# Issuing the next pair's probabilities and scores ahead of the turned outputs of pairs 0 and 1, and layer 1's gate rows behind two head units

## The reference, cut to what matters

```
mod = cond @ w_mod[l] + b_mod[l]                  # six vectors of 1024
h = rms_norm(x, norm_mix[l]) * (1 + sc_a) + sh_a
mq, mk, mv, dq, dk, dv = split(h @ w_in[l])       # 12 units of 256 columns
q, k = partial_rope(rms_norm(q)), partial_rope(rms_norm(k))
o_m = rms_norm(softmax(mq mk^T, causal) @ mv)     # 8 heads of 64
o_d = rms_norm((softmax_1 - lam * softmax_2) @ dv) # 4 double heads, values 128 wide
x = x + g_a * (concat(o_m, o_d) @ w_out[l])
h = rms_norm(x, norm_ffn[l]) * (1 + sc_f) + sh_f
x = x + g_f * ((silu(h @ w_gate[l]) * (h @ w_up[l])) @ w_down[l])
```

## Time and profile before

| what | value |
|---|---|
| median of 3 runs | 2172.64 us (2172.41 to 2173.16) |
| the profiled execution's own time | 2173.13 us |
| its span, first to last instruction | 2171.4 us |
| tensor engine (PE) busy | 2092.4 us, 96% |
| VectorE (DVE) busy | 875.6 us, 40% |
| ScalarE (ACT) busy | 374.7 us, 17% |
| mean granted clock of the tensor engine | 0.984 of full speed |
| layer 0's attention stage of the second block | about 1410 to 1557 us of the span |
| layer 1's attention stage of the second block | about 1790 to 1945 us of the span |

### The profile page before, as it was taken

The page is one execution under the profiler, slowest core; times in us unless marked ns, Lnnn a source line. Parts: engine busy times, 40 slices in busy tenths (PEclk is TensorE's granted clock), DMA queues, the critical chain, the costliest instruction groups (busy, mean ns, idle before and its releaser), DMA issues.

```text
span 2171.4 us, 37454 instructions
## 1 busy us (share of the span) xinstructions
PE 2092.4 (96%) x16270; PEld 1553.5 (72%) x16270; DVE 875.6 (40%) x1693; ACT 374.7 (17%) x899; POOL 74.5 (3%) x180
## 2 busy tenths in 40 slices
PE   8998999999999989999999999999999999999998
PEld 8786786887788867866653554388687768868786
DVE  1414525677734154242010000135566754454443
ACT  1312240000013122401010000133300012431000
POOL 3000000010000000020000000000000010000000
PEclk9999899999999998998999999999999999999999
DMA  9334234598563342327999999962568754333452
GB/s 261 97 98 153 90 126 151 182 322 277 194 197 98 97 160 78 126 79 235 348 312 377 345 347 326 315 212 97 176 238 291 265 182 151 98 117 120 154 174 97
DMA packets 333831, 421.44 MB, mean 194 GB/s; under 512 B 27222, under 2 KB 282148, under 8 KB 333668
## 3 DMA queue, kind: packets, MB, share of 16 engines
q1 hardware_dynamic: 312464, 352.96, 50.3%
q0 software_dynamic: 13408, 50.66, 6.6%
q10 hardware_dynamic: 7796, 15.43, 2.0%
HBM read 417.90 MB, written 1.05 MB: 193 GB/s over the span
## 4 chain that ended last, share of the span: by engine, by line
PE 84%; DMA 6%; DVE 4%; ACT 3%; ACTq 1%; issue 1%; SPq 0%; DVEq 0%
PE psum L1295 15%; PE psum L1327 13%; PE psum L1434 11%; PE psum L1302 9%; PE psum L1312 9%; PE psum L1494 5%; DMA ring<-in_w_up 4%; PE psum L1958 3%; PE psum L1565 3%; PE psum L1740 2%; PE psum L1339 2%; DMA ring<-in_ffn_w 2%; ACTq L653 1%; PE psum L1423 1%; PE psum L1507 1%
## 5 line engine op out<-in xcount | busy, mean ns | idle before, releaser
L1295 PE MATMUL psum<-xT,ring 128*128 128x256 f32 x1600 | 373.7, 394 | 6.8 <-ACT small L779 4.1
L1295 PEld LDWEIGHTS psum<-xT,ring 128*128 128x128 f32 x1600 | 312.1, 197 | 63.1 <-issue 7.0
L1312 PE MATMUL psum<-ring,arena 128*128 128x512 f32 x528 | 232.1, 593 | 0.0
L1302 PE MATMUL psum<-ring,xT 128*128 128x256 f32 (+2 forms) x960 | 201.1, 367 | 2.8 <-DVE arena L2466 2.1
L1302 PEld LDWEIGHTS psum<-ring,xT 128*128 128x128 f32 x960 | 170.6, 190 | 29.4 <-DVE arena L2466 2.7
L1312 PEld LDWEIGHTS psum<-ring,arena 128*128 128x128 f32 x528 | 97.9, 190 | 111.8 <-issue 111.6
L2145 DVE SCALAR_TENSOR_TENSOR arena<-arena,cond 128x512 f32<-128x512 f32 x168 | 126.2, 751 | 5.5
L1327 PEld LDWEIGHTS psum<-xT,ring 128*128 128x128 f32 x960 | 112.8, 194 | 20.7 <-issue 20.7
L1434 PE MATMUL psum<-ring,arena 128*32 128x256 f32 x2304 | 126.8, 379 | 0.7 <-DVE arena L2299 0.7
L1327 PE MATMUL psum<-oT,arena 128*128 128x128 f32 x960 | 117.4, 275 | 5.9 <-DVE arena L2160 5.8
L1327 PE MATMUL psum<-xT,ring 128*128 128x128 f32 x960 | 114.1, 278 | 6.0 <-DMA ring<-in_w_up 3.5
(11 more groups left out here) (414 smaller groups left out, 2518.4 us busy)
## 6 DMA issues: line engine op xcount, KB each, us to landing
ring<-in_w_in SPq DMA_DIRECT2D x80, 1024.0 KB, 5.5
ring<-in_exp_w SPq DMA_DIRECT2D x312, 256.0 KB, 6.2
arena<-in_w_mod POOLq DMA_DIRECT2D x48, 1024.0 KB, 9.2
ring<-in_ffn_w SPq DMA_DIRECT2D x33, 1024.0 KB, 7.3
arena<-in_exp_w SPq DMA_DIRECT2D x120, 256.0 KB, 7.1
ring<-in_w_gate SPq DMA_DIRECT2D x22, 1024.0 KB, 7.6
ring<-in_w_up SPq DMA_DIRECT2D x22, 1024.0 KB, 10.1
ring<-in_w_down SPq DMA_DIRECT2D x22, 1024.0 KB, 5.0
```

The lines of the kernel that those rows point to most:

```text
L1295: ins = pe.matmul(dst, w[:, k * 256 + c0:k * 256 + c0 + m], act_t[:, k, :], start=(k == 0), stop=(k == KT - 1))
L1302: ins = pe.matmul(dst, xT[:, k, t * P:t * P + P], w[:, k * 256 + c0:k * 256 + c0 + n], start=(k == 0), stop=(k == KT - 1))
L1312: ins = pe.matmul(psum[:, 4 + 2 * t + h, :], gT[:, s % 2, f * 256 + t * P:f * 256 + t * P + P], w2[:, f * D + h * 512:f * D + h * 512 + 51 ...
```

## The change

On the tensor engine, in both layers: `turn_probs2(l, 2)` and `scores2(l, 3)` go ahead of `turn_outs(l, 0)` and `weigh2(l, 1)`; `turn_probs2(l, 3)` goes ahead of `turn_outs(l, 1)` and `weigh2(l, 2)`. ScalarE's list follows: `keep_probs(l, 2)` ahead of `keep_outs(l, 0)`, `keep_probs(l, 3)` ahead of `keep_outs(l, 1)`. In layer 1 alone: `spread(1)` goes behind `project(1, 2)`, `keep_clock` stands ahead of that projection and has 6 products in place of 14, and ScalarE's `keep_rows(1)` goes behind the roots of the first two head units. VectorE, GpSimd and SP issue the same instructions in the same order. Line numbers from L1092 on are higher by 1 to 4 in the changed file.

```diff
                 act.preload_act_table_set("natural_log_exp_and_others")
-                keep_rows(l)
+                if l == 0:
+                    keep_rows(l)
...
                 square_heads(l, 1)
                 head_roots(l, 1)
+                if l == 1:
+                    keep_rows(l)
                 keep_heads(l, 0)
...
                 keep_heads(l, 6)
+                keep_probs(l, 2)
                 keep_outs(l, 0)
                 square_outs(l, 1)
-                keep_probs(l, 2)
                 out_roots(l, 1)
                 exp2(l, 3)
                 keep_values(l, 8)
                 keep_heads(l, 7)
+                keep_probs(l, 3)
                 keep_outs(l, 1)
                 square_outs(l, 2)
-                keep_probs(l, 3)
                 out_roots(l, 2)
...
+                del turned_last[:]
+                if l == 1:
+                    keep_clock(3, 6)
+                project(l, 2)
                 if l == 1:
                     spread(1)
-                    keep_clock(3, 14)
-                del turned_last[:]
-                project(l, 2)
                 turn_heads(l, 0)
...
                 turn_heads(l, 6)
+                turn_probs2(l, 2)
+                scores2(l, 3)
                 turn_outs(l, 0)
                 weigh2(l, 1)
-                turn_probs2(l, 2)
-                scores2(l, 3)
                 project(l, 8)
                 turn_heads(l, 7)
+                turn_probs2(l, 3)
                 turn_outs(l, 1)
                 weigh2(l, 2)
-                turn_probs2(l, 3)
                 project(l, 9)
```

## The result

The changed kernel took 2158.87 us (median of 5 runs, 2158.04 to 2160.52), the kernel before 2172.41 in the same series (5 runs, 2167.36 to 2173.16): ratio 0.9949, 95% interval 0.9936 to 0.9961. That is 11 us or 0.5% less at the ratio, and more than forecast; the time lies 2.5 us under the low end of the range. The two runs of the kernel before that joined the first three were 2167.36 and 2171.18, so its times spread over 5.8 us and not over the 0.75 that the first three showed. The profiled execution of the changed kernel took 2160.52.

A forecast was written before the change was run, and what follows sets the result against it. The tensor engine, busy for 96% of the span, was taken as the bound. Gains of 2.28 (layer 0), 3.89 (layer 1's pairs and clock) and 3.16 (layer 1's start) sum to 9.33 us: median 2163.3, range 2161.4 to 2165.9.

The forecast's parts named there:

- Pair 0's and pair 1's gaps: Tensor engine's idle gaps before these pairs' turned outputs: moved work fits in, gaining 1.62 and 0.66 us per layer.
- Layer 1's clock: Layer 1, turned heads to next projection: the clock no longer falls behind pair 0's shortened gap, gaining 1.61 us.
- Layer 1's start: Gate rows to turned heads of unit 0: 11.86 us in place of 15.02, gaining 3.16.
- The six identity products: Products kept ahead of layer 1's projection: they hide nothing and cost their 1.41 us in full.
- The sum: Layer 0's 2.28, layer 1's pairs and clock 3.89, and layer 1's start 3.16 make 9.33 us.
- the level: Starting time of the whole kernel: profiled execution 2173.13 us, 0.49 above the median of 2172.64.
- the 0.8 that the range allowed: Whole kernel: the part of the range, in us, set aside for the spread of three runs.
- Rival 2: Layer 0's dense stage: one clock fall fewer behind its wait, 1.71 us more gain, 2161.6 us; chance 0.07.
- more idle time at that load: Dense stages: longer tensor engine idle time at a load would show the forecast wrong; loads were priced at cost 0.
- Rival 1: Reordered pairs: the lower clock keeps its place or takes another, gain 7.72 us, 2164.9 us; chance 0.17.
- Rival 3: Pairs: moved work doesn't fit, so they give nothing and only 3.16 us is left, 2169.5 us; chance 0.07.
- Rival 4: Four reordered places: clock falls for long stretches, 10.3 us slower, 2182.9 us; chance 0.02.

The follow-up runs named there:

- the pairs alone: Only the reordering at pairs 0 and 1 in both layers, layer 1's start left as before, against the kernel before: 2163.69 us, ratio 0.9963.
- r3_before: The kernel before, unedited, run and profiled once more in the third later series: ratio 0.9997, times 2165.06 to 2173.34 us.
- r1_head: Only the change at layer 1's start, pairs left as before, against the kernel before: 2166.37 us, ratio 0.9984.

## Why the prediction was right or wrong

*Pair 0's and pair 1's gaps, right.* Forecast 1.62 and 0.66, measured 5.96 - 4.35 = 1.61 and 0.92 - 0.26 = 0.66. Layer 0's stage without a fall went from 146.80 to 144.50, 2.30, against 2.28. No new wait came at the moved probabilities or at the copies on ScalarE.

*Layer 1's clock, right in the place it spoke of.* 1.61 forecast for the fall. Filling the gap took 155.37 to 153.76, 1.61; the pairs alone took 3.80 to 3.85 out of the stage, against 3.89. By the Trainium skill's page "TensorE: Matmul & The Clock Gate" (section on HAM oscillation), which ties the return to the lower clock to longer idle gaps, this fall would have stayed. The runs decide against it for gaps of 2.0 to 2.2 us, filled, shortened and put back.

*Layer 1's start, right and slightly under.* 3.16 forecast, 3.34 measured (11.68 us in place of 15.02); the projection took 6.91 and the identity products 1.34, against 7.01 and 1.41. The six identity products were said to hide nothing and to cost 1.41; taking them away brought 1.1.

*The sum, right for what it summed.* The two stages gave 9.5 us in the profiles, against 9.33.

*What failed is the step from the sum to the time.* Two terms of it were wrong: the level that the 9.33 us are taken from, and layer 0's clock, which had no term at all.

First, the level. "2173.13, 0.49 above the median of 2172.64" took three runs within 0.75 us as the kernel's level and its spread. The 67 single times of the kernel before in the three later series run from 2162.79 to 2175.88 with a median of 2170.34. The starting point was 2.3 us too high. That was the luck of three runs, but the 0.8 that the range allowed for their spread was far too little: the first block alone varies by 6.8, and the medians of the three series lie between 2169.47 and 2171.17.

Second, the falls. I read the fall in layer 1 and its absence in layer 0 as properties of the two places, so the sum removed one fall of 1.61. With the 2.21 gap, layer 0's stage had a fall of 3.2 in two of four profiles (r3_before and r1_head). So by an estimate from these four its gap costs 1.6 on average, which the profile on which the sum rests did not contain. The change removes that too. Rival 2 had the right idea, that a gap may or may not be punished, and hung it on the wrong place, the load in the dense stage, which goes on varying in both kernels. The forecast named more idle time at that load as a sign of being wrong. It came in two of three profiles of the changed kernel (3.42 and 3.17 us, against 2.83), but the kernel before shows 1.57 to 3.24 too, so it is no effect of the change that these profiles can show.

With these the account comes to 2163.3 forecast, less 2.3 of level, less 1.6 of layer 0's falls, less 0.15 of the sum, 2159.25; the 17 times of the changed kernel have a median of 2159.28. That it meets within 0.03 is luck. The 1.6 is two falls in four profiles and could as well be 0.8 or 2.4; how often the clock falls in layer 0 stays open. Nor do the times alone show this term: the repeat of the changed kernel gave 10.9 us with an interval of 7.4 to 14.5, which holds the 9.5 of the stages too. The profiles show it. That the first series showed 13.5 us between its medians, and the later ones 10.9 and 10.5, is what medians of five runs do with such a spread; the interval of its ratio (8.5 to 13.9 us) holds them all.

*The rivals.* Rival 1 (the fall stays) is excluded by the clock of 1.00 in three profiles. Rival 3 (no room) is excluded by the rows above. Rival 4 (long falls) didn't come; it spoke of four stretches, where the earlier trace rows shows three windows.

## What to carry to other kernels

A profile is one draw. Before a gain of a few microseconds is set against a time, look at how far single executions of the same kernel lie apart, and time a copy of it against itself; lengths of stages that wait for no load repeated within 0.05 us here but for the falls, and show a gain of 1 us that the total hides.

Where an idle gap of about 2 us on the tensor engine stands in busy surroundings, price it at its length plus a chance of the lower clock behind it, in every place that has such a gap and not only where the one profile shows the fall. And before moving work into a gap, ask which instruction on the other engine releases it: here one copy moved ahead of a square and two roots took 1.35 us out of each gap.

## What was new about the hardware

The same 2.21 us gap was followed by a fall of the granted clock in all four profiles in layer 1, at 1.6 us each, and in two of the four in layer 0, at 3.2 us each. So one profile without a fall doesn't say that a gap is free. Gaps of 0.4 to 0.9 us in the same place (seven profiled executions, two layers each) were followed by no fall, nor were 88 idle times of up to 1.73 us elsewhere in the second block. Filling the gap with products that nothing reads made the kernel 4.8 us faster at the ratio (2.2 to 7.4).
